# Four reorderings around the feed-forward blocks of a streaming encoder: where the conv tails are turned, where the norm block stands, and the order of ScalarE's and VectorE's first work

## The chip, the cores and the metric

The kernel runs on one core of one Trainium2 chip. The metric is the device time of one launch in microseconds, of the slowest core (there is one here). All numbers are for fp32 data. Engines: TensorE does matmuls and transposes, VectorE and ScalarE work on elements, GpSimd does some sums here, SyncE issues nearly all DMAs.

## The reference

One step of an encoder with two layers, for 1024 prompt tokens and 8 streams of 16 tokens, 1152 tokens in all, width 1024. Layer 0 has a recurrent mixer with a pooling mixer, layer 1 a chunked MLP mixer. Each layer ends in the block that the change is about, a gated feed-forward of width 2816 with a causal convolution of width 3:

```
h = rms_norm(x, norm_ffn[layer])
proj = einsum('btd,df->btf', h, w_in)          # width 2 * 2816
a, gate = proj[..., :D_FF], proj[..., D_FF:]
full = concatenate([conv_hist, a], axis=1)
conv = conv_b + sum(full[:, j:j + T] * conv_w[j] for j in range(3))
y = einsum('btf,fd->btd', gelu(conv) * gate, w_out)
new_state = full[:, -2:]                       # the last two rows of a: an output
x = x + y
```

`new_state`, the last two rows of `a` of every stream, is an output (`conv_prompt`, `conv_sample`). The kernel calls it the tails.

## The kernel before

All activations lie transposed: features on the 128 partitions, the 1152 tokens along the free axis. x is `xs`, 8 blocks (d = 0 to 7) of 128 features. For norms and mixers the tokens are in three blocks of 384 (tb = 0, 1, 2); in the feed-forward they are in two halves of 576 (T1S, T2S). Each fp32 operand is split in a high part (rounded to fp32r by ScalarE, an ACT Copy) and a low part (the rest, a VectorE subtraction), and each product is three matmuls: high x high, high x low, low x high. So every operand passes through ScalarE and then VectorE before TensorE can take it.

The feed-forward `ffn(l)` uses a seven-product scheme on 2 x 2 blocks, with sums of weight blocks (`fraw`, `flf`) and of activation blocks. The up part has 22 pairs of feature blocks with 7 products each (154 positions, `pos`). The first 14 positions are the **head**: pairs n = 0 and 1 interleaved, q in the order 1, 2, 3, 7, 5, 6, 4 and n = 0, 1 in each. A product has four k, each of six matmuls of 288 columns. In the head the operands are formed while the products already run. The down part has 7 products (j = 0 to 6, in the order 2, 1, 5, 3, 6, 4, 7) of STEPS = 11 steps (step r = 11 j + kk); a step has f = 0 to 3 with six matmuls each, and f has the PSUM banks `psp[f]`. After each j VectorE adds the four results to `xs` (`down_evict`), two instructions for each f at j = 0, one at j = 4. TensorE does steps kk = 0 and 1 of a j together, f by f: f = 0 of both, f = 1 of both, and so on. It starts f = 0 of a new j as soon as f = 0 of the old one is evicted (`d_out`).

The order on every engine is written out by hand and each engine runs its instructions in program order; engines wait for one another by counting semaphores. What the change touches:

- **tail_sq(l, d, tb) and rms(k, tb, b)** on ScalarE (lines 3248 and 2893). TensorE and GpSimd sum squares of x over features; tail_sq is the square of one block, once VectorE has added the last product to it; rms takes the sum that TensorE has made over the partitions and makes rstd by Ln and Exp. VectorE's first multiplication in the feed-forward, `normed(0, T1S)`, needs rms of blocks 0 and 1, since T1S reaches into block 1.
- **norm_block(l, 2, ssq)** on TensorE (line 1095, called in `passes`): two matmuls with ones, the first over the sum of the squares, the second over the last square. The second half of the tokens hangs on it.
- **head_evict(n, what)** on VectorE: results of the head. "a" is a sum (`keepa`), "c22" needs "a"; TensorE's product (n, q = 4) writes the banks that "c22" of the same n has read. `combo_low(5, k)` forms the low parts of the operand of the products q = 4.
- **turn_tails(l)** on TensorE: four transposes of `tails` into bank 7, half of `psp[3]`, so between the eviction of f = 3 of one j and the first matmul of f = 3 of the next. **tail_rows(l)** on ScalarE copies them out into `trow` (four copies), **store_tails(l)** on SyncE stores them with four DMAs. TensorE's f = 3 waits for the copies (`trow_ready`). SyncE issues the weight loads of step r (`step_weights(r)`) some steps ahead of their use.

ScalarE's loop in the down part is, for each r: `w_high(r)`, `y_high(r)`, then what is tied to that r. VectorE's, for most r: `w_sum(r + 1)`, `y_sum(r + 1)`, `w_low(r)`, `y_low(r)`; at the first steps of a j another order:

```
j, kk = divmod(r + 1, STEPS)
if kk == 2 and j:
    w_low(r)
    y_low(r)
    down_evict(j - 1)
    w_sum(r + 1)
    y_sum(r + 1)
elif kk == 3 and j:
    w_low(r)
    y_low(r)
    w_sum(r + 1)
    y_sum(r + 1)
```

With kk of r + 1, the evictions of j = 0 stand behind the low parts of r = 12, and the sums of r = 14 behind the low parts of r = 13.

Of the kernel before, what the change touches and what calls it, by code (L numbers as in the profile page):

```python
# [39 lines left out]
STEPS = FJ // 2  # L40
# [45 lines left out]
def build(nc, A, O):  # L86
    ctx = ExitStack()
    with ctx:
# [431 lines left out]
        def parted(l, x, k):  # L520
# [5 lines left out]
        HEAD_ACT = ((0, "p1"), (1, "p1"), (0, "c11"), (1, "c11"), (0, "e3"), (1, "e3"))  # L526
        HEAD_DVE = ((0, "d"), (1, "d"), (0, "a"), (0, "c22"), (1, "a"), (0, "c12"), (1, "c22"), (1, "c12"),
                    (0, "c21"), (1, "c21"))
# [165 lines left out]
        def _(sp):  # L694
# [101 lines left out]
            def ffn(l):  # L796
# [97 lines left out]
                for r in range(5, DOWNS):  # L894
# [5 lines left out]
                    if r == 7:  # L900
                        y_tiles(yb22[:, 5:9, :], 16, 20, T2S, y_back[2])
                    if r == 5 * STEPS + 9:
                        store_tails(l)
# [94 lines left out]
        def _(pe):  # L998
# [521 lines left out]
            def turn_tails(l):  # L1520

                pe.wait_ge(conv_step[l], 9 * FJ)
                pe.wait_ge(d_out, 28 * l + 20)
                flat = tails[:, :, :].rearrange("p r f -> p (r f)")
                for b, (c0, c1) in enumerate(((0, 44), (44, 172), (172, 300), (300, 396))):
                    mm = pe.transpose(ps[7][0:c1 - c0, b * P:(b + 1) * P], flat[:, c0:c1], ident[:, :])
                mm.then_inc(tails_mm, 1)
# [13 lines left out]
            def ffn(l):  # L1541
# [11 lines left out]
                def passes(pos, bank, q, first):  # L1553

                    n = pos // 7 if pos >= 14 else 0
                    for k in range(4):
# [4 lines left out]
                        for e, (w, part) in enumerate(((fh, 0), (fh, 1), (fl, 0))):  # L1561
                            for c in range(2):
                                mm = pe.matmul(bank[:, M0 + c * CH:M0 + (c + 1) * CH], w[:, pos % RING, k * P:(k + 1) * P],  # L1563
                                               x[:, m, part, c * CH:(c + 1) * CH], start=first and k == 0 and e == 0,
                                               stop=k == 3 and e == 2, skip_group_check=True)
                        if pos == 0 and k == 1:
                            norm_block(l, 2, ssq_b if l else ssq_e)
# [54 lines left out]
                def down_step(r, f):  # L1622
# [7 lines left out]
                    if kk == 0:  # L1630
# [6 lines left out]
                        else:  # L1637
                            pe.wait_ge(up_dve_out, on_dve(l, PAIRS - 1, (C21, C12)[f]))
                    if r == 5 * STEPS and f == 3:
                        pe.wait_ge(trow_ready, 4 * (l + 1))  # L1640
# [11 lines left out]
                for j in range(7):  # L1652
                    r0 = STEPS * j
                    for first, last in ((0, 2), *((k, k + 1) for k in range(2, STEPS - 2)), (STEPS - 2, STEPS)):
                        for f in range(4):
                            for kk in range(first, last):
                                down_step(r0 + kk, f)
                            if j == 5 and first == 0 and f == 1:
                                turn_tails(l)
                            if l and j == 6 and last == STEPS and f:  # L1660
                                finish(f - 1)
# [120 lines left out]
        def _(dve):  # L1782
# [429 lines left out]
            def ffn(l):  # L2212
# [259 lines left out]
                def at_first(tb, d0, d1):  # L2472

                    for d in range(d0, d1):
                        (down_tail if l else abo_tail)(d, tb)
# [12 lines left out]
                def late_tile():  # L2488

                    nonlocal late  # L2490
                    d = first + late
                    at_first(2, d, d + 1)
                    late += 1
# [53 lines left out]
                up_low(11)  # L2547
                up_low(12)
                dve.memset(apad_a[:, 0:2], 0.0)
                dve.memset(apad_b[:, 0:2], 0.0)  # L2550
                head_evict(0, "a")
                head_evict(0, "c22")
                for k in range(4):
                    combo_low(5, k)
                head_evict(1, "a")
                up_low(13)
# [311 lines left out]
        def _(act):  # L2868
# [414 lines left out]
            def ffn(l):  # L3283
# [110 lines left out]
                for d in range(first, KD):  # L3394
                    tail_sq(l, d, 1)
                rms(k, 0, 6 + 1)
                rms(k, 1, 6)
                tail_sq(l, first, 2)
                for x in range(4):
# [87 lines left out]
                for r in range(2, DOWNS):  # L3487
# [5 lines left out]
                    j, kk = divmod(r, STEPS)  # L3493
                    if r == 5 * STEPS + 2:
                        tail_rows(l)
# [392 lines left out]
```

## Time and profile before

| what | value |
|---|---|
| median of 3 runs | 2673.71 us (2672.64 to 2676.48) |
| the profiled execution | 2672.64 us, its span 2670.9 us |
| TensorE busy | 2626.0 us, 98% of the span |
| VectorE busy | 1845.8 us, 69% |
| ScalarE busy | 937.7 us, 35% |
| GpSimd busy | 275.8 us, 10% |
| mean granted TensorE clock | 0.998 |
| DMA | 249.01 MB, 93 GB/s over the span |

Layer 0's feed-forward head begins near 510 us and its down part at 1010 us; layer 1's lie near 1906 us and 2406 us. The span is counted from the first instruction to the last of the core; the execution's own time is 1.7 us longer. Times in the rows are from the start of the span. An idle time in brackets is that of the engine just before the row, with what ended it; gaps under about 0.2 us are not shown.

### The profile page before, as it was taken

The numbers are of one execution on the slowest core, as the hardware profiler recorded it, in microseconds if no ns is written. First come the engines' busy times: TensorE is split into PE (matmuls) and PEld (weight loads), VectorE is DVE, ScalarE is ACT, GpSimd is POOL, SyncE is SP. The second block draws the span as 40 slices with busy tenths as digits, with TensorE's granted clock in tenths as the row PEclk, the third lists the DMA queues.
The fourth block names the chain that finished last, engine by engine and source line by source line (L and its number), as shares of the span: only waits on it lengthen the run. The fifth ranks groups of instructions, "written<-read, shape, count | busy, mean of one in ns | idle before, by whom it ended". The sixth has DMA issues, their size and how long they took to land.

```text
span 2670.9 us, 45385 instructions
## 1 busy us (share of the span) xinstructions
PE 2626.0 (98%) x17820; PEld 2555.6 (96%) x17820; DVE 1845.8 (69%) x3093; ACT 937.7 (35%) x1550; POOL 275.8 (10%) x255
## 2 busy tenths in 40 slices
PE   9999999999999999999999999999999999999998
PEld 8989999999999999999888999999899999999998
DVE  3548985697777779788323755445787777779787
ACT  4414454433232324345322211213433232334344
POOL 3234325100000000000000330001300000000000
PEclk9999999999999999999999999999999999999999
DMA  5112002222222248634111111112222222248643
GB/s 154 40 32 56 24 20 64 97 62 75 75 75 75 75 142 289 233 129 127 37 50 54 44 40 40 42 43 66 88 73 77 73 78 73 78 157 300 205 129 138
DMA packets 236722, 249.01 MB, mean 93 GB/s; under 512 B 13099, under 2 KB 176116, under 8 KB 236276
## 3 DMA queue, kind: packets, MB, share of 16 engines
q1 hardware_dynamic: 236500, 246.36, 28.6%
q8 instruction: 132, 2.16, 0.3%
q14 instruction: 58, 0.48, 0.1%
q10 hardware_dynamic: 32, 0.01, 0.0%
HBM read 202.12 MB, written 44.20 MB: 92 GB/s over the span
## 4 chain that ended last, share of the span: by engine, by line
PE 87%; DVE 7%; issue 2%; ACT 2%; DMA 1%; SPq 0%; DVEq 0%; POOL 0%; ACTq 0%; POOLq 0%
PE banks L1563 34%; PE banks L1644 16%; PE banks L1018 11%; PE banks L1690 7%; PE banks L1043 6%; PE banks L1208 3%; PE banks L1494 1%; PE banks L1068 1%; PE banks L1243 1%; PE banks L1515 1%; PE banks L1146 1%; PE banks L1749 1%; DMA fraw<-in_w_out_ffn 1%; DVE cx L2278 1%; DVE xs L2253 1%
## 5 line engine op out<-in xcount | busy, mean ns | idle before, releaser
L1563 PE MATMUL banks<-cx,fh 128*128 128x288 f32 x2816 | 486.7, 294 | 1.2 <-issue 0.4
L1563 PEld LDWEIGHTS banks<-cx,fh 128*128 128x128 f32 x2816 | 411.7, 188 | 3.1 <-ACT cw L3312 1.6
L1563 PE MATMUL banks<-cw,fh 128*128 128x288 f32 x2112 | 364.9, 294 | 10.4 <-ACT fh L3301 4.7
L1563 PEld LDWEIGHTS banks<-cw,fh 128*128 128x128 f32 x2112 | 308.6, 188 | 12.5 <-issue 7.7
L1563 PE MATMUL banks<-cx,fl 128*128 128x288 f32 x1408 | 300.0, 294 | 0.0
L1644 PE MATMUL banks<-ysh,fh 128*128 128x288 f32 x1232 | 265.0, 296 | 1.9 <-DVE ysl L2445 0.9
L1644 PE MATMUL banks<-ysl,fh 128*128 128x288 f32 x1232 | 262.0, 293 | 0.0
L1644 PE MATMUL banks<-ysh,fl 128*128 128x288 f32 x1232 | 261.0, 293 | 0.0
L3301 ACT ACTIVATE fh<-fraw 128x512 fp32r<-128x512 f32 x220 | 138.4, 631 | 341.9 <-PE banks L1563 289.0
L1563 PE MATMUL banks<-cw,fl 128*128 128x288 f32 x1056 | 225.0, 294 | 0.0
L1563 PEld LDWEIGHTS banks<-cx,fl 128*128 128x128 f32 x1408 | 224.3, 187 | 0.0
L2877 ACT ACTIVATE wh<-raw 128x512 fp32r<-128x512 f32 x104 | 65.5, 629 | 383.6 <-PE banks L1018 212.6
L1644 PEld LDWEIGHTS banks<-ysh,fh 128*128 128x128 f32 x1232 | 195.7, 187 | 3.5 <-issue 3.5
L1644 PEld LDWEIGHTS banks<-ysl,fh 128*128 128x128 f32 x1232 | 197.3, 188 | 0.0
L1644 PEld LDWEIGHTS banks<-ysh,fl 128*128 128x128 f32 x1232 | 196.6, 187 | 0.0
L2249 DVE TENSOR_TENSOR fl<-fraw,fh 128x512 fp32r<-128x512 f32 x220 | 151.6, 691 | 63.9 <-ACT fh L3301 63.9
L1563 PEld LDWEIGHTS banks<-cw,fl 128*128 128x128 f32 x1056 | 168.2, 187 | 0.0
L1806 DVE TENSOR_TENSOR xs<-banks,xs 128x384 f32<-128x384 f32 x192 | 96.5, 550 | 99.9 <-PE banks L1043 46.1
L1786 DVE TENSOR_TENSOR wl<-raw,wh 128x512 fp32r<-128x512 f32 x104 | 85.8, 825 | 112.0 <-ACT wh L2877 112.0
L3367 ACT ACTIVATE fh<-flf 128x512 fp32r<-128x512 f32 x110 | 69.6, 633 | 194.9 <-DVE flf L2428 194.8
L3675 POOL TENSOR_TENSOR raw<-raw,vec 128x512 f32<-128x512 f32 x72 | 86.1, 1202 | 454.0 <-DMA raw<-in_w_uv_c 376.4
L1018 PE MATMUL banks<-xh,wh 128*128 128x384 f32 x552 | 126.4, 336 | 0.0
(432 smaller groups left out, 5190.1 us busy)
## 6 DMA issues: line engine op xcount, KB each, us to landing
fraw<-in_w_out_ffn SPq DMA_DIRECT2D x264, 256.0 KB, 3.3
fraw<-in_w_in_ffn SPq DMA_DIRECT2D x176, 256.0 KB, 4.3
y_scratch<-gate SPq DMA_DIRECT2D x44, 576.0 KB, 3.3
raw<-in_w_uv_c SPq DMA_DIRECT2D x64, 256.0 KB, 2.7
yb<-y_scratch SPq DMA_DIRECT2D x10, 1440.0 KB, 8.9
raw<-in_w_in_ab SPq DMA_DIRECT2D x40, 256.0 KB, 2.9
raw<-in_w_out_c SPq DMA_DIRECT2D x32, 256.0 KB, 2.7
xs<-x_scratch SPq DMA_DIRECT2D x2, 2304.0 KB, 10.1
```

The costliest lines, as they stand in the source:

```text
L1018: mm = pe.matmul(ps[(sg + tb) % BANKS][:, 0:TB], w[:, place, k * P:(k + 1) * P], r[:, kk, tbs(tb)], start=kk == 0 and c == 0, stop=kk == K ...
L1043: mm = pe.matmul(ps[(sg + g0 + tb) % BANKS][:, 0:TB], w[:, place, k * 256 + dd * P:k * 256 + (dd + 1) * P], r[:, k, tbs(tb)], start=k == 0 ...
L1208: mm = pe.matmul(ps[beside_bank(j, tb)][:, 0:TB], w[:, h, k * P:(k + 1) * P], r[:, kk, tbs(tb)], start=first, stop=last)
L1563: mm = pe.matmul(bank[:, M0 + c * CH:M0 + (c + 1) * CH], w[:, pos % RING, k * P:(k + 1) * P], x[:, m, part, c * CH:(c + 1) * CH], start=fi ...
L1644: mm = pe.matmul(psp[f][:, M0 + c * CH:M0 + (c + 1) * CH], w[:, f * P:(f + 1) * P], x[:, r % RINGD, c * CH:(c + 1) * CH], start=kk == 0 an ...
L1690: mm = pe.matmul(ps[g % BANKS][:, :], x[:, k, t * P:(t + 1) * P], w, start=k == 0 and e == 0, stop=k == KD - 1 and e == 2)
L1786: dve.tensor_tensor(wl[:, s % 2, :], raw[:, s % RAWS, :], wh[:, s % 2, :].bitcast(F32), ALU.subtract)\
L1806: dve.tensor_tensor(xs[:, d, tbs(tb)], ps[sg % BANKS][:, 0:TB], xs[:, d, tbs(tb)], ALU.add)\
L2249: dve.tensor_tensor(fl[:, pos % RING, :], src, fh[:, pos % RING, :].bitcast(F32), ALU.subtract)\
L3301: act.activation(fh[:, pos % RING, :], src, ACT.Copy).then_inc(f_high, 1)
L3367: act.activation(hi, src, ACT.Copy).then_inc(f_high, 1)
L3675: pool.tensor_tensor(r, r, g, ALU.mult).then_inc(w_scaled, 1)
```

## The change

Six small moves, in both layers, with no change of what is computed:

- ScalarE: the first square of block 2 stands between rms of block 0 and rms of block 1, and not behind both.
- TensorE: norm_block of block 2 comes after k = 0 of product 0, and not after k = 1.
- VectorE: in the head, `combo_low(5, ...)` stands ahead of both "a" evictions, both of these and the two memsets ahead of "c22" of n = 0; HEAD_DVE, which numbers the evictions, follows.
- TensorE, ScalarE, SyncE: the tails are turned in the first steps of j = 1 and not of j = 5; their copies stand behind y_high of r = 14 (STEPS + 3) and not of r = 57 (5 STEPS + 2); their stores behind the weights of r = 20 and not of r = 64.
- `late_tile` is written without the name d; it does the same.

```diff
-        HEAD_DVE = ((0, "d"), (1, "d"), (0, "a"), (0, "c22"), (1, "a"), (0, "c12"), (1, "c22"), (1, "c12"),
+        HEAD_DVE = ((0, "d"), (1, "d"), (0, "a"), (1, "a"), (0, "c22"), (0, "c12"), (1, "c22"), (1, "c12"),
...
-                    if r == 5 * STEPS + 9:
+                    if r == 20:
                         store_tails(l)
...
             def turn_tails(l):
 
                 pe.wait_ge(conv_step[l], 9 * FJ)
-                pe.wait_ge(d_out, 28 * l + 20)
+                pe.wait_ge(d_out, 28 * l + 4)
...
-                        if pos == 0 and k == 1:
+                        if pos == 0 and k == 0:
                             norm_block(l, 2, ssq_b if l else ssq_e)
...
-                    if r == 5 * STEPS and f == 3:
+                    if r == STEPS and f == 3:
                         pe.wait_ge(trow_ready, 4 * (l + 1))
...
-                            if j == 5 and first == 0 and f == 1:
+                            if j == 1 and first == 0 and f == 1:
                                 turn_tails(l)
...
                 up_low(12)
+                for k in range(4):
+                    combo_low(5, k)
+                head_evict(0, "a")
+                head_evict(1, "a")
                 dve.memset(apad_a[:, 0:2], 0.0)
                 dve.memset(apad_b[:, 0:2], 0.0)
-                head_evict(0, "a")
                 head_evict(0, "c22")
-                for k in range(4):
-                    combo_low(5, k)
-                head_evict(1, "a")
                 up_low(13)
                 head_evict(0, "c12")
...
                 rms(k, 0, 6 + 1)
+                tail_sq(l, first, 2)
                 rms(k, 1, 6)
-                tail_sq(l, first, 2)
...
-                    if r == 5 * STEPS + 2:
+                    if r == STEPS + 3:
                         tail_rows(l)
```

## Rows read from the trace of the kernel before

**Rows 1.** The page: busy time of the engines, and one line of the DMA issues (KB each, us to landing).

```profile
PE 2626.0 (98%) x17820; PEld 2555.6 (96%) x17820; DVE 1845.8 (69%) x3093; ACT 937.7 (35%) x1550; POOL 275.8 (10%) x255
...
fraw<-in_w_out_ffn SPq DMA_DIRECT2D x264, 256.0 KB, 3.3
```

**Rows 2.** Stretches: us, then busy time of PE, PEld, DVE, ACT, POOL, PEclk, DMA.

```profile
160.00:165.00 5.00, 5.00 (x19) 4.02 (x19) 1.09 (x1) 1.01 (x2) 4.68 (x3) 0.66 0.00 0
...
580.00:1010.00 430.00, 430.00 (x3254) 430.00 (x3253) 314.05 (x527) 129.99 (x195) 0.00 (x0) 1.00 0.29 90
```

**Rows 3.** TensorE's timeline, head of layer 0: start us, us, instructions, idle before.

```profile
514.71 0.91 PE L1106 MATMUL banks<-sq_t,ones 128*128 128x384 f32 x2 [1.61 <-ACT sq_t L3259]
...
561.87 0.77 PE L1563 MATMUL banks<-cw,fh 128*128 128x288 f32 x4 [1.08 <-issue]
...
575.45 0.77 PE L1563 MATMUL banks<-cw,fh 128*128 128x288 f32 x4 [0.65 <-ACT fh L3301]
```

**Rows 4.** VectorE's timeline, head of layer 0.

```profile
502.34 3.80 DVE L2253 SCALAR_TENSOR_TENSOR xs<-xs,vec,rstd 128x576 f32<-128x576 f32 x4
...
516.84 3.00 DVE L2253 SCALAR_TENSOR_TENSOR xs<-xs,vec,rstd 128x576 f32<-128x576 f32 x4 [0.73 <-ACT rstd L2901]
...
521.74 2.77 DVE L2278 TENSOR_TENSOR cx<-xs,cx 128x576 fp32r<-128x576 f32 x4 [0.58 <-ACT cx L3312]
```

**Rows 5.** ScalarE's timeline, head of layer 0.

```profile
499.26 0.58 ACT L2898 ACTIVATE rstd<-banks,vec 128x384 f32<-128x384 f32 x1 [0.71 <-PE banks L1106]
...
499.87 0.53 ACT L2901 ACTIVATE rstd<-rstd 128x384 f32<-128x384 f32 x1
...
502.45 0.53 ACT L3259 ACTIVATE sq_t<-xs 128x384 f32<-128x384 f32 x1 [2.05 <-DVE xs L1806]
...
520.41 0.65 ACT L3336 ACTIVATE p1b<-banks 128x576 f32<-128x576 f32 x1 [2.00 <-PE banks L1563]
```

**Rows 6.** VectorE's timeline, head of layer 0, the evictions before product 12.

```profile
554.65 0.75 DVE L2292 TENSOR_TENSOR u<-banks,p 128x576 f32<-128x576 f32 x1
...
555.50 0.82 DVE L2305 TENSOR_TENSOR apad_b<-banks,u 128x448 f32<-128x448 f32 x2
...
556.24 2.75 DVE L2278 TENSOR_TENSOR cw<-cwf,cw 128x576 fp32r<-128x576 f32 x4
...
560.91 0.75 DVE L2305 TENSOR_TENSOR gate<-banks,a 128x576 f32<-128x576 f32 x1
```

**Rows 7.** TensorE, VectorE and ScalarE, down stage of layer 0, j = 0 to 1.

```profile
1010.27 0.43 PE L1644 MATMUL banks<-ysh,fh 128*128 128x288 f32 x2
...
1054.43 0.43 PE L1644 MATMUL banks<-ysh,fl 128*128 128x288 f32 x2
...
1055.09 0.50 PE L1644 MATMUL banks<-ysh,fh 128*128 128x288 f32 x2 [0.23 <-DVE ysl L2445]
...
1042.95 5.40 DVE L2465 TENSOR_TENSOR xs<-xs,banks 128x576 f32<-128x576 f32 x8
...
1051.65 0.75 DVE L2589 TENSOR_TENSOR yslf<-yb,yb 128x576 f32<-128x576 f32 x1
...
1052.43 0.69 ACT L3386 ACTIVATE ysh<-yslf 128x576 fp32r<-128x576 f32 x1
```

**Rows 8.** TensorE and ScalarE at j = 5; SyncE's waits, 1000 to 1260 us.

```profile
1189.62 0.60 PE L1526 MATMUL banks<-ident,tails 128*44 128x128 f32 x4
...
1189.98 0.51 PE L1644 MATMUL banks<-ysh,fh 128*128 128x288 f32 x2
...
1190.26 0.75 ACT L3280 ACTIVATE trow<-banks 44x128 f32<-44x128 f32 x4 [1.47 <-PE banks L1526]
...
SPq L787 <- ACT trow L3280: 7.7, 1, 7.7
```

**Rows 9.** ScalarE and VectorE, head of layer 1.

```profile
1892.33 0.53 ACT L3259 ACTIVATE sq_t<-xs 128x384 f32<-128x384 f32 x1
...
1892.38 2.31 DVE L2253 SCALAR_TENSOR_TENSOR xs<-xs,vec,rstd 128x576 f32<-128x576 f32 x2
```

More of the change, by code:

```diff
@@ L2490, in late_tile @@
                     nonlocal late
-                    d = first + late
-                    at_first(2, d, d + 1)
+                    at_first(2, first + late, first + late + 1)
                     late += 1
```

## The prediction

> **What bounds the kernel now.** I read the page first. TensorE is busy 98% of the span [rows 1], so only what lengthens or shortens TensorE's idle time can move the end. Then the table by stretches [rows 2]: from 580 to 1010 us TensorE is busy all 430.00 us with 3254 matmuls, 0.132 us each, so six matmuls (one k of a product, or one f of a down step) take 0.79 us. The idle time that the change can touch is at the start of each feed-forward block (the head, where 14 products run while the operands are still being formed), and there I read TensorE's timeline [rows 3]: 1.61 us before the last norm matmul, 1.08 us before product 13, 0.65 us before product 17. These are the first and the last two of eight gaps of 0.2 us or so between 510 and 580, which add up to 7.3 us; layer 1 repeats the pattern. After 575.45 the next gap is at 1055.09, of 0.23 us [rows 7]. Next who sets the head's pace: VectorE's timeline [rows 4] has gaps of 0.2 us or more between 502.34 and 575 at two places only, 0.73 us (waiting for ScalarE's rstd) and 0.58 us (for ScalarE's cx). Everything else is back to back. So in the head a delay of VectorE's first instruction is a delay of TensorE at the end of the head, unless one of these two gaps takes it in.
>
> **1. ScalarE: the square of block 2 goes ahead of rms of block 1.** Now ScalarE computes Ln at 499.26 and Exp at 499.87, done at 500.40, and only then waits 2.05 us for VectorE's add and squares at 502.45 [rows 5]. VectorE's first normed, at 502.34, needs that Exp and finds it long done. Turned round, Ln and Exp stand behind the square, which waits for the add that ends at 502.4. The square takes 0.53 us, with up to 0.1 of it under the start of the next instruction, so I take 0.45; from the start of Ln to that of Exp it is 0.61, and Exp takes 0.53: rstd is ready at 502.45 + 0.45 + 0.61 + 0.53 = 504.04. Normed starts at 504.04 and not 502.34: +1.70 us. Behind it in VectorE's queue stand the late adds of block 2; the square of the last of them, the norm matmul and rstd let it start the second half at 516.84; all of it moves by 1.70. In layer 1 the square now runs at 1892.33 and normed at 1892.38 [rows 9]; with the square first, normed starts near 1893.92: +1.54. The squares of block 2 gain nothing: the first was not what the norm waits for, the last was.
>
> **2. TensorE: the norm block after k = 0 and not after k = 1 of product 0.** Its second matmul waits for the last square (1.61 us, [rows 3]), so it doesn't start earlier. But one k, 0.79 us, that was done before the wait now comes behind it. Product 0 and product 1 end 0.79 later counted from the norm. ScalarE takes product 1's bank at 520.41 as soon as it is done, waiting 2.00 us for TensorE [rows 5], and combo_high(6) is queued behind that; VectorE waits for it already, 0.58 us at 521.74 [rows 4]. So this wait grows to 1.37 and VectorE's chain is 0.79 late, in each layer. If ScalarE could go ahead by itself the cost would be nothing; if the norm did come earlier the gain is at most the idle 0.73 before 516.84. The row of 520.41 says it can't, so I take 0.79.
>
> **3. VectorE: both "a" evictions, and c22 of n = 0, behind combo_low(5).** Work is the same. The wait of c22 on "a" just before it goes: 554.65 to 555.50 is 0.85 where the usual pitch of such an instruction is 0.67, so 0.17 us is saved [rows 6]. Against it, product 12 (n 0, q 4) waits for c22, now done by 556.32 and in time. With combo_low (4 x 0.67) and two evictions (2 x 0.67) ahead from 554.65 it starts at 558.66 and ends at 559.48; TensorE can start 0.2 later (c22 of n = 1 starts at 560.91, ends 0.75 later, TensorE starts at 561.87: 0.21), at 559.69, where it now starts product 12 at 557.6 (561.87 less the gap of 1.08 and a product of 3.17). Then product 13 follows at 562.95 instead of 561.87, and product 17, four products of 3.17 later, at 575.63 instead of 575.45: +0.18, since its old gap of 0.65 takes in the rest [rows 3]. Layer 1: the same. Bounds: from -0.17 (if product 12 finds c22 in time) to +1.08 (if the later gap didn't absorb).
>
> Head: 1.70 + 0.79 + 0.18 = 2.67 us in layer 0, 1.54 + 0.79 + 0.18 = 2.51 in layer 1.
>
> **4. The conv tails are turned in down product j = 1, not j = 5.** At j = 5 ScalarE stands idle 1.47 us waiting for the transposes and copies them at once (four copies, 0.75 us in all, 1190.26 [rows 8]); TensorE's steps f = 2 cover that, and it has no gap. At j = 1 the order is another. TensorE starts the down stage at 1010.27 [rows 7]; 11 steps of 3.17 bring it to 1045.2, f = 0 and f = 1 of the first two steps to 1048.4. The new wait is for all four evictions of j = 0, which VectorE makes in eight instructions from 1042.95, 5.40 us long [rows 7], to 1048.35: in time within 0.1. Then transposes, 0.36 us (1189.62 to 1189.98 [rows 8]), and f = 2 until 1050.4. Then f = 3 waits for the four copies, and those stand in ScalarE's queue behind w_high and y_high of r = STEPS + 3 = 14. y_high(14) needs VectorE's y_sum(14), at 1051.65, which stands behind the evictions and the parts of r = 13; ScalarE makes it at 1052.43, 0.69 long [rows 7]. The copies run from 1053.0 to 1053.75 and f = 3 starts at 1053.9. In the old kernel it started at 1045.2 + 6 x 0.79 = 1049.98. That is +3.92. It gives back the hiccup at 1055.09 (VectorE was just late with r = 14; from 1054.43 to the next start it is 0.66 there, where two matmuls take 0.26), 0.39, and the transposes of j = 5, 0.36: net +3.17. Layer 1 issues the same instructions on the same shapes, and I take the same. Nothing downstream can give this back: TensorE is the bound of the rest of the stage. Bounds: 0 if the copies were in time; 4.3 with no hiccup recovered and the transposes not got back.
>
> SyncE's store_tails goes from r = 64 to r = 20. It now blocks SyncE 7.7 us [rows 8], without a gap of TensorE near it, so freeing it gains nothing. At r = 20 the copies are done, and its four DMAs go in between weight loads that are some steps ahead of VectorE. I cost them at 0, and at most at 1 us a layer, an estimate: a weight load of 256 KB lands in 3.3 us [rows 1], the four stores together are smaller, and what they push is only partly waited for.
>
> Sum: 2.67 + 2.51 + 2 x 3.17 = **+11.5 us**. Against the profiled execution's 2672.64 that is 2684.2; the median of the runs is 1.07 above it, which gives 2685.2. I say **2685**.
>
> **Rivals.**
> *The clock falls in the new gaps.* Behind the gap of 1.61 us the clock stays at full speed, as in all of the span from there on. Once in this trace it doesn't: 160 to 165 us has a mean grant of 0.66 [rows 2], 1.7 us of full-speed work lost at the level of 1.2 GHz, in a stage with small matmuls and many waits. My new gaps in the down stage are 3.5 us long, twice that one. If each costs 1.7 us: 2685 + 3.4 = 2688.4. In the head the new idle is cut in two by the first norm matmul. The Trainium skill ("TensorE: Matmul & The Clock Gate", section on HAM oscillation) says that waits between bursts of matmuls can put the clock back to its low level each time; by that rule it would be this case; no row of this trace has a gap long enough to say.
> *Only the head bites.* If ScalarE reaches the tail copies in time, say because VectorE sums r = 14 sooner, what is left is 5.2: 2678.9. Against it: 1052.43 is a start of an instruction that the copies follow in program order.
> *Only the down stage bites*, since a slack in the head that I don't see absorbs 1 and 2: 2680.1. Against it: VectorE's unbroken rows.
> *Not slower.* The earlier norm and the reordered evictions close VectorE's two gaps in the head (0.73 + 0.58, twice), and the copies are in time: 2.6 us less, 2671.1. It decides if the last square is done before TensorE reaches the norm, at 511.5; now it is done at 514.7, and edit 1 makes it later.
> *The tail stores push the weights*: +1 a layer, 2687.
>
> **How the numbers follow.** Forecast as summed: 0.60, and its own range 2683 to 2687. Clock 0.10, pushed weights 0.08, only the down stage 0.07, only the head 0.10, not slower 0.05. The range 2680 to 2690 leaves out the last two, 0.15. A measurement of this kernel tells 0.2% from no change, 5.3 us, that is 2668.4 to 2679.1. Faster: 0.02 (not slower, with other gaps closed too). Same: 0.03 + 0.10 = 0.13. Slower: 0.85.
>
> **What would show it.** VectorE's first normed (L2253) 1.7 us after the add before it; a gap of TensorE before the norm's first matmul too; VectorE's wait for cx at 1.4 us; a gap of some 2.2 us before product 12; in the down stage a gap of about 3.5 us before f = 3, in each layer, ended by ScalarE's trow, and none at the transposes. I am wrong if the trow gap is absent or short, if the second k of product 0 isn't what delays ScalarE, or if the grant drops behind the gaps.

## The result, and the profile after

The changed kernel takes 2690.89 us (median of 4 runs, 2688.49 to 2691.95), the kernel before beside it 2673.18 us (2672.09 to 2676.48): ratio 1.0063, 95% interval 1.0045 to 1.0081, +17.7 us by the medians. The forecast was slower, by 11.5 us; the time lies 0.9 us above the range of 2680 to 2690. The profiled execution took 2691.84 us.

The page of the changed kernel, its first rows, beside [rows 1]:

```profile
span 2690.1 us, 45385 instructions
...
PE 2636.1 (98%) x17820; PEld 2565.1 (95%) x17820; DVE 1847.9 (69%) x3093; ACT 937.6 (35%) x1550; POOL 273.7 (10%) x255
```

The counts are those of before, yet TensorE is busy 10.1 us longer: the same 17820 matmuls ran slower somewhere. Idle time alone would leave this number as it was. Of the 19.2 us that the span has grown (2670.9 to 2690.1), 10.1 are busy time of TensorE and 9.1 idle time. GpSimd's busy time is 2.1 us less. TensorE's timeline has the gaps (start, length, instructions, idle before), to be held against [rows 3, 7]. The first six rows are layer 0, the others layer 1:

```profile
512.86 0.91 PE L1102 MATMUL banks<-ssq_e,ones 128*128 128x384 f32 x2 [0.90 <-POOL ssq_e L3680]
515.90 1.65 PE L1106 MATMUL banks<-sq_t,ones 128*128 128x384 f32 x2 [2.12 <-ACT sq_t L3258]
...
564.32 0.76 PE L1563 MATMUL banks<-cw,fh 128*128 128x288 f32 x4 [2.05 <-issue]
...
1058.64 0.82 PE L1644 MATMUL banks<-ysh,fh 128*128 128x288 f32 x2 [3.22 <-ACT trow L3279]
1059.26 0.69 PE L1644 MATMUL banks<-ysl,fh 128*128 128x288 f32 x2
1059.74 0.69 PE L1644 MATMUL banks<-ysh,fl 128*128 128x288 f32 x2
...
1919.75 0.91 PE L1102 MATMUL banks<-ssq_b,ones 128*128 128x384 f32 x2 [1.70 <-POOL ssq_b L3680]
...
1921.39 1.65 PE L1106 MATMUL banks<-sq_t,ones 128*128 128x384 f32 x2 [0.73 <-ACT sq_t L3258]
...
2464.49 0.82 PE L1644 MATMUL banks<-ysh,fh 128*128 128x288 f32 x2 [3.22 <-ACT trow L3279]
```

The gaps of TensorE that the forecast named are there: one before the norm's first matmul, 2.05 before product 12 (forecast 2.2) with none left before 13 and 17, and 3.22 before f = 3 (forecast 3.5). What the forecast did not have is the length of the work behind them: the norm's two matmuls take 1.65 us where they took 0.91, and behind f = 3's gap a pair of matmuls starts 0.48 us after the pair before it (1059.26, 1059.74), where a pair at full clock takes 0.26. The table by stretches shows it (us, busy time of PE, PEld, DVE, ACT, POOL, then PEclk, the granted share of the 2.4 GHz, where 0.50 is 1.2 GHz):

```profile
515.00:520.00 5.00, 4.10 (x14) 3.50 (x15) 3.54 (x6) 2.05 (x4) 0.00 (x0) 0.50 0.11 39
520.00:525.00 5.00, 5.00 (x33) 5.00 (x33) 2.45 (x4) 1.17 (x2) 0.00 (x0) 0.83 0.00 0
...
1055.00:1060.00 5.00, 1.78 (x10) 1.57 (x9) 2.11 (x4) 2.03 (x7) 0.00 (x0) 0.76 0.44 149
1060.00:1065.00 5.00, 5.00 (x24) 5.00 (x24) 4.44 (x8) 2.46 (x4) 0.00 (x0) 0.56 0.27 88
...
1920.00:1925.00 5.00, 4.27 (x15) 3.05 (x15) 2.87 (x6) 2.05 (x4) 0.00 (x0) 0.66 0.22 79
...
1970.00:1975.00 5.00, 5.00 (x31) 5.00 (x31) 4.47 (x8) 0.63 (x1) 0.00 (x0) 0.76 0.19 56
...
2465.00:2470.00 5.00, 5.00 (x32) 5.00 (x31) 3.59 (x6) 1.64 (x3) 0.00 (x0) 0.77 0.10 31
```

Read x: TensorE, busy all 5.00 us, does 24 matmuls from 1060 to 1065 and 40 in a like stretch at full clock (1050 to 1055). Behind each of the new gaps but the one before product 12 in layer 0 the clock is low for a few us. The kernel before, at full clock behind its gap of 1.61 us and behind two of 1.76 us (before 539.76 and 1935.41), shows nothing of the kind in the heads and down parts.

VectorE's timeline answers to [rows 4], first two rows of the head:

```profile
502.17 0.56 DVE L1806 TENSOR_TENSOR xs<-banks,xs 128x384 f32<-128x384 f32 x1 [4.90 <-PE banks L1515]
504.34 3.01 DVE L2253 SCALAR_TENSOR_TENSOR xs<-xs,vec,rstd 128x576 f32<-128x576 f32 x4 [1.62 <-ACT rstd L2900]
```

Counted from the transposes ahead of the head, which are 0.31 us later here, normed starts 1.70 us late, as forecast. But its four instructions take 3.01 us, not 3.80: half of the delay comes back at once. GpSimd's timeline, of before and then of after, and between them VectorE's of before, show what is different:

```profile
503.05 1.01 POOL L3681 TENSOR_TENSOR ssq_e<-ssq_e,sq_t 128x384 f32<-128x384 f32 x1 [9.24 <-ACT sq_t L3259]
```

```profile
503.06 1.62 DVE L2253 SCALAR_TENSOR_TENSOR xs<-xs,vec,rstd 128x576 f32<-128x576 f32 x1
```

```profile
503.36 1.01 POOL L3680 TENSOR_TENSOR ssq_e<-ssq_e,sq_t 128x384 f32<-128x384 f32 x1 [9.25 <-ACT sq_t L3258]
```

Before, this add ran from 503.05 to 504.06, inside normed (from 502.34), and the one normed instruction that started beside it took 1.62 us, where the others take 0.81; after, it is over at 504.37, as normed starts. I come back to this with the last experiments.

For the sum I compare positions of TensorE's landmarks in two traces: the transposes of the conv taps ahead of each head, the first matmul of each down part, the first matmul behind it (layer 0) or the first final transpose (layer 1). The kernel after has the first two at 510.29 and 1015.01, the one before at 509.98 and 1010.27 [rows 7]: 504.72 less 500.29 is +4.43 for the head and up part of layer 0. In this way:

| us more than before | head and up, 0 | down, 0 | head and up, 1 | down, 1 |
|---|---|---|---|---|
| the change | +4.43 | +5.46 | +4.68 | +4.25 |
| forecast | +2.67 | +3.17 | +2.51 | +3.17 |
| square first alone (e1) | +2.43 | 0.01 | +0.76 | 0.22 |
| norm after k = 0 alone (e2) | +2.36 | -0.71 | +0.78 | +2.46 |
| VectorE's order alone (e3) | +1.62 | 0.04 | +0.10 | +1.03 |
| tails at j = 1 alone (e4) | -0.01 | +5.49 | -0.01 | +3.53 |
| the change, two gaps a layer filled (e5) | +1.94 | +2.36 | +1.76 | +2.33 |
| tails at j = 1, gap filled (e8) | 0.02 | +2.87 | 0.02 | +2.00 |
| tails at j = 1, copies one step earlier (e7) | 0.00 | -0.34 | 0.01 | +0.39 |
| squares on TensorE (e11) | -0.59 | 0.27 | +0.53 | 0.04 |
| square first and norm after k = 0 (e6) | +3.20 | +0.71 | +3.10 | +1.06 |
| squares on TensorE in layer 0, and the pair of "a" (e13) | -0.79 | -0.72 | -0.18 | -1.19 |

Each row is one profiled execution. A stretch that an experiment doesn't touch moves by up to 0.7 us, in the last column by up to 1.2, and once, in e2, by 2.46. Where no edit reaches, ahead of the first head, it varies as well: the transposes there start between 0.95 us earlier and 2.17 us later than in the kernel before. The low stretch near 160 us [rows 2] is longer in e1, e3, e6 and e7 (1.88 to 2.17 us later) and missing in the change, e2, e4, e8 and e11.

### The profile page after: what moved, and what is told of

Its sections match the earlier page's. It is cut to its first block, busy times and chain, and to the rows that moved or that the text cites. A ratio compares the mean times of both kernels' runs of the same rounds, so it can differ in the third digit from the quotient of the medians.

```text
span 2690.1 us, 45385 instructions
## 1 busy us (share of the span) xinstructions
PE 2636.1 (98%) x17820; PEld 2565.1 (95%) x17820; DVE 1847.9 (69%) x3093; ACT 937.6 (35%) x1550; POOL 273.7 (10%) x255
## 4 chain that ended last, share of the span: by engine, by line
PE 88%; DVE 7%; issue 2%; ACT 2%; DMA 1%; DVEq 0%; SPq 0%; POOL 0%; ACTq 0%; POOLq 0%
PE banks L1563 35%; PE banks L1644 17%; PE banks L1018 11%; PE banks L1690 7%; PE banks L1043 6%; PE banks L1208 3%; PE banks L1494 1%; PE banks L1068 1%; PE banks L1515 1%; PE banks L1243 1%; PE banks L1146 1%; PE banks L1749 1%; DVE xs L2253 1%; DVE qsc L1917 1%; DVE cx L2278 0%
## 6 DMA issues: line engine op xcount, KB each, us to landing
xs<-x_scratch SPq DMA_DIRECT2D x2, 2304.0 KB, 10.1
```

## The experiments

**Each edit alone.** e1, on the kernel before:

```diff
                 rms(k, 0, 6 + 1)
-                rms(k, 1, 6)
                 tail_sq(l, first, 2)
+                rms(k, 1, 6)
```

> The kernel before with edit 1 alone (ScalarE's first square of block 2 ahead of rms of block 1). The changed kernel's trace has VectorE's first normed 1.69 us later, but its four instructions in 3.01 us where they took 3.80. Theory A (the waits are as forecast except that VectorE gets part back while GpSimd's sum isn't beside it, and the clock falls where gaps of TensorE add up): the last late add is 0.9 us later, the norm gap about 2.5 us instead of 1.6, layer 0's up part 0.9 us longer and layer 1's 0.9 to 1.5; with the clock at full speed +2 us in all, with it fallen behind the gap up to +3 more a layer. Theory B (the waits cost what the forecast says, the clock costs nothing): 1.70 + 1.54 = +3.2 us, at full clock.

Measured: 2676.62 us beside 2672.80, ratio 1.0010 (1.0000 to 1.0019). The head of layer 0 is 2.43 longer, that of layer 1 0.76. Its stretches, layer 0 and then layer 1, and the gaps of TensorE:

```profile
515.00:520.00 5.00, 2.88 (x10) 1.97 (x10) 4.20 (x8) 3.06 (x6) 0.00 (x0) 0.85 0.11 39
520.00:525.00 5.00, 5.00 (x33) 5.00 (x33) 3.58 (x5) 1.53 (x3) 0.00 (x0) 0.81 0.00 0
...
1913.00:1918.00 5.00, 3.37 (x18) 2.34 (x17) 3.60 (x6) 1.85 (x4) 1.00 (x1) 1.00 0.21 79
```

```profile
517.78 0.98 PE L1106 MATMUL banks<-sq_t,ones 128*128 128x384 f32 x2 [2.12 <-ACT sq_t L3259]
...
1914.05 0.91 PE L1102 MATMUL banks<-ssq_b,ones 128*128 128x384 f32 x2 [0.90 <-POOL ssq_b L3681]
```

Layer 1 is the pure wait: normed 1.5 late, and 0.76 of it given back (its first pair takes 1.55 us, [rows 9] has 2.31), so 0.76 is left of the 1.54 of step 1. In layer 0 normed is 1.70 late and takes 3.00 for 3.80, so 0.90 by waits; the other 1.5 goes with the low grant of 0.85 and 0.81 in its two stretches. The ten times fall in two groups, four of 2671.62 to 2673.34 and six of 2676.22 to 2678.46, with nothing between: the first theory's range holds, but the whole price is not paid in each execution.

e2, `if pos == 0 and k == 1` made `k == 0` on the kernel before:

```diff
-                        if pos == 0 and k == 1:
+                        if pos == 0 and k == 0:
```

> The kernel before with edit 2 alone (norm block of block 2 after k = 0). Both theories: one k of 0.79 us goes from before the gap to behind it; gap 2.4 us in layer 0 and 1.5 in layer 1, VectorE's wait for cx 1.37 us instead of 0.58, +0.79 us a layer, +1.6. Theory A adds: if the clock falls behind the 2.4 us gap of layer 0, up to 3 us more there. Rival: the norm matmul gets done earlier and the half starts earlier: 0 or less.

Measured: 2676.50 beside 2672.80, ratio 1.0011 (1.0001 to 1.0020). +0.78 in the head of layer 1, one k of 0.79, as step 2 said. But the delay does not come where step 2 and the expectation put it. VectorE's wait for cx stays at 0.58 us, in both layers (in the changed kernel too), and there is a new one of 0.82 us ahead of flf, a sum of weight blocks whose code waits for an earlier product (`f_done`). It starts 0.05 us after ScalarE has begun to take product 1's bank (1917.61), so VectorE waits here for product 1 directly and no longer finds it done. VectorE's timeline, layer 1:

```profile
1917.66 0.69 DVE L2238 TENSOR_TENSOR flf<-fraw 128x512 f32<-128x512 f32 x1 [0.82 <-issue]
...
1918.93 2.76 DVE L2278 TENSOR_TENSOR cx<-xs,cx 128x576 fp32r<-128x576 f32 x4 [0.58 <-ACT cx L3312]
```

Layer 0 is 2.36 longer; the gap and the clock behind it are:

```profile
513.84 1.65 PE L1106 MATMUL banks<-sq_t,ones 128*128 128x384 f32 x2 [2.13 <-ACT sq_t L3259]
```

```profile
510.00:515.00 5.00, 2.86 (x11) 1.69 (x10) 5.00 (x7) 2.49 (x4) 0.74 (x1) 0.88 0.19 69
515.00:520.00 5.00, 5.00 (x31) 4.72 (x30) 3.30 (x6) 2.70 (x5) 0.00 (x0) 0.78 0.00 0
```

In its last stage there is a gap of 1.88 us ended by VectorE's `xs`, with a grant of 0.67 behind it, where before had 0.65 us. The edit doesn't reach there, and why VectorE was later isn't settled.

The head of layer 1 has a low stretch too, behind a gap of 1.77 us that every trace has there:

```profile
1936.95 1.13 PE L1563 MATMUL banks<-cw,fh 128*128 128x288 f32 x4 [1.77 <-ACT fh L3301]
```

```profile
1936.00:1941.00 5.00, 4.05 (x19) 4.08 (x20) 5.00 (x9) 2.77 (x5) 0.00 (x0) 0.66 0.21 57
```

It cost nothing: VectorE is busy all 5.00 us there, and from 1936.95 to the first matmul behind the next gap of over 1 us (1959.06) it is 22.11 us, the same as in e1 at full clock (1940.74 to 1962.85). TensorE's small waits for VectorE and ScalarE on this way took the slower matmuls in.

e3, VectorE's order alone (the HEAD_DVE line and the moved calls of the diff):

```diff
+                for k in range(4):
+                    combo_low(5, k)
+                head_evict(0, "a")
+                head_evict(1, "a")
                 dve.memset(apad_a[:, 0:2], 0.0)
                 dve.memset(apad_b[:, 0:2], 0.0)
-                head_evict(0, "a")
                 head_evict(0, "c22")
-                for k in range(4):
-                    combo_low(5, k)
-                head_evict(1, "a")
```

> The kernel before with edit 3 alone (VectorE's order before product 12). Both theories: a gap of 2.0 us before product 12 and none before product 13 (1.08 now) nor before 17 (0.65), +0.2 us a layer, +0.4 in all, if the clock holds. Theory A: in the changed kernel the clock fell for a while from just after this gap in layer 1 and not in layer 0, so here it may fall in either, for up to 1.7 us each.

Measured: 2676.39 beside 2672.80, ratio 1.0014 (1.0004 to 1.0024). Layer 1 is 0.10 longer at full clock (step 3 said 0.18); layer 0 is 1.62 longer with a grant of 0.75 behind the same gap:

```profile
561.57 0.77 PE L1563 MATMUL banks<-cw,fh 128*128 128x288 f32 x4 [2.06 <-issue]
```

```profile
560.00:565.00 5.00, 3.43 (x17) 3.46 (x18) 4.91 (x12) 0.24 (x1) 0.00 (x0) 0.75 0.54 153
...
1955.00:1960.00 5.00, 2.94 (x23) 2.73 (x21) 5.00 (x13) 0.63 (x1) 0.00 (x0) 1.00 0.73 209
```

e4, the tails at j = 1 alone, copies and stores as in the change:

```diff
-                    if r == 5 * STEPS + 9:
+                    if r == 20:
                         store_tails(l)
...
-                pe.wait_ge(d_out, 28 * l + 20)
+                pe.wait_ge(d_out, 28 * l + 4)
...
-                    if r == 5 * STEPS and f == 3:
+                    if r == STEPS and f == 3:
...
-                            if j == 5 and first == 0 and f == 1:
+                            if j == 1 and first == 0 and f == 1:
...
-                    if r == 5 * STEPS + 2:
+                    if r == STEPS + 3:
                         tail_rows(l)
```

> The kernel before with edit 4 alone (tails turned at j = 1, copied behind r = 14, stored at r = 20). Theory A: a gap of 3.2 us ended by ScalarE's trow in each layer, grant near 0.5 for a few us behind it: each down part 4.2 to 5.5 us longer, +8.5 to +11 us, mean clock 0.996 or less. Theory B: gap 3.2 us, clock 1.00, 3.2 us longer each: +6.3. Theory C (the stores push the weights): gaps behind waits for weights in the rest of j = 1, ended by the DMA.

Measured: 2680.72 beside 2672.80, ratio 1.0030 (1.0019 to 1.0042): +7.9, between the 6.3 of the second theory and the 8.5 at the lower end of the first. The gap is 3.23 us in both layers. Behind it the clock differs:

```profile
1050.00:1055.00 5.00, 2.04 (x8) 2.07 (x9) 1.58 (x4) 1.96 (x6) 0.00 (x0) 0.78 0.50 184
1055.00:1060.00 5.00, 5.00 (x35) 5.00 (x35) 5.00 (x9) 2.64 (x4) 0.00 (x0) 0.88 0.34 104
...
2450.00:2455.00 5.00, 1.77 (x14) 1.57 (x13) 2.54 (x4) 2.46 (x7) 0.00 (x0) 1.00 0.73 266
2455.00:2460.00 5.00, 5.00 (x40) 5.00 (x40) 4.75 (x8) 2.64 (x4) 0.00 (x0) 1.00 0.30 97
```

This trace has two more gaps, at the start of j = 2 in each layer, ended by VectorE's additions, where before has 0.20 and 0.65 us and the changed kernel none:

```profile
1085.87 0.50 PE L1644 MATMUL banks<-ysh,fh 128*128 128x288 f32 x2 [1.05 <-DVE xs L2465]
...
2485.49 0.51 PE L1644 MATMUL banks<-ysh,fh 128*128 128x288 f32 x2 [1.03 <-DVE xs L2465]
```

Such a gap comes and goes from trace to trace, and no run shows why.

The four medians add up to 3.8 + 3.7 + 3.6 + 7.9 = 19.0, and the change costs 17.7: additive as far as medians with intervals of 2 to 3 us either way can tell (that of e1 begins at no change).

**Is it the clock? The gaps filled.** e5 is the changed kernel with matmuls of no use in its gaps: 18 ahead of the norm block, into a bank that the norm block overwrites, and 22 ahead of the wait for the tails' copies. They use operands that are ready, and nobody reads them.

```diff
+                            pe.wait_ge(rms_ready, NTB * (1 + 2 * l) + 2)
+                            for e in range(18):
+                                pe.matmul(ps[6][:, 0:CH], fh[:, 0, 0:P], cx[:, 0, 0, 0:CH], start=True, stop=True,
+                                          skip_group_check=True)
                             norm_block(l, 2, ssq_b if l else ssq_e)
...
                     if r == STEPS and f == 3:
+                        for e in range(22):
+                            pe.matmul(psp[3][:, M0:M0 + CH], ring(r)[0][:, 0:P], ysh[:, r % RINGD, 0:CH],
+                                      start=True, stop=True, skip_group_check=True)
                         pe.wait_ge(trow_ready, 4 * (l + 1))
```

> The changed kernel with idle matmuls in TensorE's gaps: 18 matmuls of 288 columns before the norm block's first matmul and 22 before the wait for trow, both into banks that are overwritten before they are read, so that TensorE works while it waits (2.4 and 2.9 us). They add work and remove no wait. Theory A (clock): the clock holds behind the filled gaps; the part behind these waits goes back to the waits alone, about 10 us over the kernel before instead of 17.7 (0.8 + 0.8 + 0.2 in each head, 3.2 to 3.5 in each down part, and up to 1.7 where the unfilled gap before product 12 still drops the clock). Theory B (no clock): the same 17.7 us or more, since the matmuls only add. Theory C (the stores push the weights): also 17.7.

Measured: 2682.95 beside 2673.65, ratio 1.0034 (1.0022 to 1.0046): 40 useless matmuls a layer more, and 8.4 us less than the change. Every execution of the changed kernel took 2688.49 us or more, with a mean grant of 0.994 or 0.995, and each of e5's six 2685.49 or less, with 0.997 or 0.998. The real work waits as before for the same things (0.20 us is left idle before f = 3), and the grant is full in every one of the stretches:

```profile
515.00:520.00 5.00, 4.10 (x28) 3.84 (x29) 4.27 (x7) 2.84 (x6) 0.00 (x0) 1.00 0.11 39
...
1055.00:1060.00 5.00, 4.80 (x37) 4.56 (x36) 2.77 (x5) 2.30 (x7) 0.00 (x0) 1.00 0.17 54
```

This splits the change. Neither of the two traces has a gap at the start of j = 2 that could blur the comparison. By the medians: 17.7 = 9.3 of waits + 8.4 of clock. By the landmarks: waits 1.94 + 2.36 + 1.76 + 2.33 = 8.4, clock 2.49 + 3.10 + 2.92 + 1.92 = 10.4, in one execution of each. The change's own trace has it as 9.1 idle and 10.1 busy.

e8 does the same to e4's edit alone (the second filler; the stores stay at r = 64).

> Edit 4 alone, with the 22 idle matmuls before the wait for trow. Theory A: clock 1.00 behind the wait in both layers, each down part 3.2 to 3.5 us longer, +6.5 to +7 us and never more behind this wait, where edit 4 without them was timed +7.9 and one layer of its trace lost 5.5. Theory B: as without them, or later by what the matmuls add.

Measured: 2677.63 beside 2673.65, ratio 1.0015 (1.0006 to 1.0025), +4.0 where the unfilled one has +7.9, and where 6.5 or more was expected. Landmarks: +2.87 and +2.00, of waits alone. The traces of e4 and e8 differ by 4.15 us in the two down parts, and not all of it is clock: the low stretch of layer 0 accounts for at most 1.7 (grants of 0.78 and 0.88 over 5 us each), and the gaps of 1.05 and 1.03 us at the start of j = 2, which e8 has not, for another 2.1. Whether the useless matmuls removed those or it was chance is open, so it is e5 that carries the reading on the clock.

**Is it the copies' place behind y_high(14)?** e7 is e4 with one thing changed:

```diff
-                    if r == 5 * STEPS + 2:
+                    if r == STEPS + 2:
                         tail_rows(l)
```

> Edit 4 alone, but ScalarE copies the tails behind y_high of r = 13 instead of 14. From the rows: y_high(13) ends 2.8 us before y_high(14), so the wait of TensorE shrinks from 3.2 us to about 0.5, each down part is 0.5 us longer or less, and the clock doesn't fall: +1 us or less in all. If the cost of edit 4 came from the transposes or the stores at j = 1 rather than from where the copies stand, it stays near +7.9.

Measured: 2673.67 beside 2673.65, ratio 1.0001 (0.9991 to 1.0010): the loss is gone. Behind y_high(13) the copies come straight after the transposes; ScalarE's timeline, and the gap of TensorE that is left:

```profile
1051.53 0.69 ACT L3386 ACTIVATE ysh<-yslf 128x576 fp32r<-128x576 f32 x1
1052.12 0.74 ACT L3280 ACTIVATE trow<-banks 44x128 f32<-44x128 f32 x4
```

```profile
1053.00 0.51 PE L1644 MATMUL banks<-ysh,fh 128*128 128x288 f32 x2 [0.45 <-ACT trow L3280]
```

So turning the tails at j = 1 costs nothing that the times (2.5 us either way) or the landmarks (-0.34 and +0.39) can tell; one step's delay of the copies in ScalarE's queue does. The stores are at r = 20 here too, so they cost nothing of note either: the rival of the pushed weights falls.

**Do the two edits at the norm share a fall of the clock?** e6 has e1's and e2's diff together.

> Edits 1 and 2 together, on the kernel before (squares first; norm block after k = 0). It asks whether the two add up, or share their stall and their low clock. Theory A (as the changed kernel showed: waits add, and the clock falls once behind the pair of gaps, not once for each edit): the head of layer 0 is 0.8 + 0.8 = 1.6 us longer by waits, plus one low stretch of 1 to 2 us; layer 1 1.5 to 1.6 by waits, up to 2 more if the clock falls there too. Beside the before: +3.2 to +7 us, so 2676 to 2680, and below the sum of the two alone (+3.8 and +3.7). Theory B (each edit costs its whole price again): 7.5 us, 2680.7. Theory C (as predicted, 1.70 + 0.79 and 1.54 + 0.79, no clock): 4.8 us, 2678, with VectorE's first normed four in 3.80 us.

Measured: 2680.12 beside 2673.14, ratio 1.0025 (1.0015 to 1.0034), +7.0. Heads: +3.20 and +3.10. By waits it is 0.90 + 0.79 and 0.76 + 0.79, so 1.7 and 1.55; the rest, 1.5 in each, is one low stretch in each head. In layer 1 neither edit alone had one at the norm; the two together have, with 1.70 and 0.73 us of idle close to one another:

```profile
1915.34 0.91 PE L1102 MATMUL banks<-ssq_b,ones 128*128 128x384 f32 x2 [1.70 <-POOL ssq_b L3681]
1916.98 0.99 PE L1106 MATMUL banks<-sq_t,ones 128*128 128x384 f32 x2 [0.73 <-ACT sq_t L3259]
```

```profile
1915.00:1920.00 5.00, 3.93 (x14) 3.02 (x15) 3.53 (x6) 2.05 (x4) 0.29 (x1) 0.77 0.22 79
```

The first of the three expectations held in the heads. The median, +7.0, is nearer to the second, since the down parts of this execution are 0.7 and 1.1 longer too; nothing of the edits is there.

**GpSimd's add beside VectorE.** e11 is the kernel before, with the last squares of block 2 summed by TensorE in the norm block (further matmuls with ones) and not by GpSimd:

```diff
                     s = tail_square(l, KD - 1, tb)
+                    if tb == 2:
+                        for q in range(s - 2 - l, s):
+                            pe.wait_ge(square_ready, TAKEN_SQ[l] + q + 1)
+                            pe.matmul(bank, ones[:, :], sq_t[:, q % 4, :], start=False, stop=False)
...
                         s = tail_square(l, d, tb)
-                        add_square(TAKEN_SQ[l] + s, added, sq_t[:, s % 4, :], tb, ssq)
+                        if tb == 2 and d >= 5 - l:
+                            pool.wait_ge(ssq_added, added)
+                            pool.sem_inc(ssq_added, 1)
+                        else:
+                            add_square(TAKEN_SQ[l] + s, added, sq_t[:, s % 4, :], tb, ssq)
```

> The kernel before, with the last squares of block 2 (two in layer 0, three in layer 1) summed by TensorE in the norm block itself (a matmul with ones each) instead of by GpSimd. It tests what made VectorE's normed instructions faster in the changed kernel: in the kernel before one of four takes 1.6 us instead of 0.8 where GpSimd's add lies beside it. Theory A (the two engines hold each other up): no normed of 1.6 us in layer 0, the last late add about 1.6 us earlier, the norm gap of 1.6 us gone or nearly, layer 0 1.3 us shorter and layer 1 0.7 or more: -2 us. Theory B (normed was slow for another reason): durations stay, and the time is the same or 0.3 longer.

Measured: 2672.56 beside 2673.65, ratio 0.9997 (0.9988 to 1.0006), where 2 us less was expected. VectorE's timeline:

```profile
501.98 3.00 DVE L2257 SCALAR_TENSOR_TENSOR xs<-xs,vec,rstd 128x576 f32<-128x576 f32 x4
...
508.04 2.99 DVE L2257 SCALAR_TENSOR_TENSOR xs<-xs,vec,rstd 128x576 f32<-128x576 f32 x4
...
515.88 3.01 DVE L2257 SCALAR_TENSOR_TENSOR xs<-xs,vec,rstd 128x576 f32<-128x576 f32 x4 [1.71 <-ACT rstd L2905]
```

Here normed starts straight behind VectorE's own add, as in the kernel before, and takes 3.00 without GpSimd's add beside it, where it took 3.80 with it. With e1 and the changed kernel, where normed starts behind the end of GpSimd's add, it shows what gave back 0.8 us of step 1. It buys little: the last late add starts 1.6 us earlier counted from the transposes (511.62 for 513.56, less 0.36 that the whole head is earlier), but now the norm block has more to do, VectorE waits 1.71 us for rstd, and layer 1 loses 0.53 where layer 0 gains 0.59.

**A try at a version that beats both.** e13: e11's edit in layer 0 alone, and of edit 3 only the part that saves the wait:

```diff
                 head_evict(0, "a")
+                head_evict(1, "a")
                 head_evict(0, "c22")
                 for k in range(4):
                     combo_low(5, k)
-                head_evict(1, "a")
```

> A try at a version that beats both: the kernel before with the last squares of block 2 summed by TensorE in layer 0 alone, and with VectorE's a of n = 1 ahead of c22 of n = 0 and both ahead of combo_low(5) (the part of edit 3 that saves the wait, without the part that makes product 12 wait). Theory A: -0.59 in layer 0's head as when it was done in both layers, and -0.17 in each layer from the pair: -0.9 us, 2672.3, with the gap before product 13 at 0.9 us and none before product 12. Theory B: the pair gives nothing, since the gap before product 17 grows by what that of product 13 loses: -0.6 us. Theory C: TensorE orders the head of layer 0 now, so nothing of the pair arrives there, and it gives 0.17 in layer 1 alone: -0.8. The time alone can't tell these apart; the shifts of TensorE's landmarks can.

Measured: 2671.99 beside 2673.14, ratio 0.9995 (0.9986 to 1.0004). The heads are 0.79 and 0.18 shorter, which is -0.6 and -0.2 in layer 0 and -0.2 in layer 1, as the first expectation had it; the gap before product 13 is 0.66 us where it had 0.9. A gain of 1 us is under what the times can tell; no version that clearly beats the kernel before was found.

## Why the prediction was wrong in size and right in direction

- **What bounds the kernel** held: every loss is a gap of TensorE or slower matmuls behind one, and the work of the other engines is the same.
- **Step 1 (+1.70, +1.54)** had the wait right and the sum wrong. Normed is late by 1.70 and by 1.53; 0.80 and 0.76 come back in normed itself, since GpSimd's add no longer runs beside it. What is left is 0.90 and 0.76. The row was on the table: [rows 4] has the first four at 3.80 and the second at 3.00, and I took them for the same work and didn't ask what the 0.80 was.
- **Step 2 (+0.79)** measured 0.78 (e2, layer 1). The size was right and the place wrong: the wait for cx did not grow to 1.4 us, it is 0.58 in e2 and in the change; VectorE lost the time ahead of flf, where it waits for product 1 itself (0.82 us) and not through ScalarE.
- **Step 3 (+0.18)** measured 0.10, the gap before product 12 2.05 for 2.2, and the later gaps took in the rest. The sum had a slip: 559.69 and 3.17 make 562.86 and not 562.95, so the step itself comes to 0.09.
- **Step 4 (+3.17)**: the gap 3.22 for 3.5, ended by ScalarE's copies behind y_high(14), and gone when they stand one step earlier (e7). Net by waits 2.36 and 2.33 (e5), 2.87 and 2.00 (e8). Next to the small gap of 0.23 at 1055.09 the gap at the start of j = 2 goes as well (0.20 us in layer 0 and 0.65 in layer 1 of before, none in e5), which I had not counted. The bound of 4.3 was too wide: with nothing given back the step is 3.92.
- **The stores (0)** held, by e7, as far as its times can tell.
- **The sum of waits**, forecast 11.5, measured 9.3 by the medians and 8.4 by the landmarks: 2 to 3 us too much.
- **The clock (rival, 0.10)** is the step that failed. It was costed at 0 in the sum, at 1.7 for each down gap in the rival. It cost 8.4 us by the medians, half of the whole, and filling the gaps gave that back (e5); so the cause is shown and not only argued. Two readings of mine were wrong. I took the full clock behind 1.61 us for a sign that new gaps cost nothing beyond their length: single gaps of 2.06 to 2.13 us had a low stretch behind them in e1, e2 and e3. And I priced the head at nothing because the new idle is cut in two there: 0.90 and 2.12 with the norm's matmul between them had the deepest stretch of all, 0.50 over 515 to 520. The Trainium skill ("TensorE: Matmul & The Clock Gate", section on HAM oscillation) had the mechanism, a return to the low level at each wait between bursts. This case agrees in part: a low stretch came behind 9 of 14 gaps of 2 us or more, not behind each. I named the rule and gave it too little weight, because I had one gap of 1.61 us at full clock as evidence, and took that as if it told of a gap of 2.1 or 3.2. Nor did the full clock hold "in all of the span from there on": the last stretch of before, 2666.00 to 2670.90, has a grant of 0.51, with TensorE idle in it, so it cost nothing.
- **Luck.** The two errors have opposite signs. The waits were forecast 2.2 us too high and the clock 8.4 too low, by the medians; that the time lies only 0.9 us above the range is owed in part to the first.
- **The rivals** of only the head, only the down part and not slower fell: both parts bite, by waits about 4 and 5 us.

What stays open: when the clock falls. The same gap of 3.23 us in the same kernel (e4) was followed by a grant of 0.78 in layer 0 and of 1.00 in layer 1; one of 2.06 us (e3) by 0.75 and by 1.00; and in the changed kernel the 2.05 us before product 12 by full clock in layer 0 and by 0.76 in layer 1. In e5 the gap before product 12 stays, 2.20 and 2.14 us, and with the others filled the clock is full behind it in both layers; layer 0:

```profile
561.80 0.77 PE L1563 MATMUL banks<-cw,fh 128*128 128x288 f32 x4 [2.20 <-issue]
```

```profile
565.00:570.00 5.00, 5.00 (x40) 5.00 (x39) 4.89 (x9) 1.27 (x2) 0.00 (x0) 1.00 0.00 0
```

Nor is 2 us a border. Of the gaps of 1.76 or 1.77 us, two in each of the twelve traces, one had a low stretch behind it (e2, layer 1), and so had one of 1.88 us (e2), but none of 1.65 and 1.67 (e6, e3). From execution to execution it varies too: e1's ten times spread from 2671.62 to 2678.46, those of e7, which has no gap over 0.7 us in the part it changes, from 2671.73 to 2674.60. The length of the gap doesn't decide it alone, and these runs don't show what does.

## What to carry to other kernels

Where TensorE is 98% busy, price a new wait of it at its length and, as a second term, at the chance of a low stretch of the clock behind it (here 1.5 to 3 us, behind 9 of the 14 gaps of 2 us or more in the heads and down parts of the change and of e1 to e6); a row that shows full clock behind a shorter gap is no evidence for a longer one. Ask too who sets the pace behind the gap: a low stretch where TensorE waits for VectorE anyway cost nothing (e2, layer 1). Before a short job is moved to another product, look at which step of the copying engine's queue it lands behind: one step of the loop was here the whole price, 7.9 us. And where the same instruction on the same shape has two durations in the profile, find out what runs beside the longer one before you sum delays: the delay may take it away.

## What the runs showed of the hardware

- Granted clock: it is low behind single gaps of 2.1 us (e1, e2, e3) and once behind 1.77 us (e2), and it is not the same for the same gap in another layer or run. Matmuls of 288 columns start 0.24 us apart at the low level (1.2 GHz, the rows of 1059.26 and 1059.74) and 0.132 apart at full clock [rows 2], so a low stretch costs close to half its length.
- 18 and 22 useless matmuls in the gaps kept the grant at 1.00 and paid for themselves: +9.3 us with them, +17.7 without. It is the better answer only where the wait can't be removed; e7 removes it.
- GpSimd's add of 1.01 us beside VectorE's normed made one of its four instructions, otherwise 0.81 us long, take 1.62 us: VectorE loses 0.8 of the 1.0 us. The Trainium skill ("SBUF — State Buffer", section "Who interferes with whom") describes an exclusive lock on ports that the two engines share, which a VectorE instruction with two inputs in SBUF contends for with a GpSimd instruction that reads SBUF. The trace agrees: the normed instruction, which reads xs and rstd, starts 0.01 us behind the add and is done only 0.6 us after it (504.68 and 504.06), and e11's 3.00 for 3.80 agrees too. Which port it is no run shows.
